# Last stage by seven half-block products (Strassen) over pairs of expert tiles, instead of eight

## The reference, cut to what matters

```python
u = u_emb[e_blk]
a = jnp.einsum('bthkd,btd->bthk', u, h_blk).astype(jnp.float32)
act = (jax.nn.gelu(a) * g_blk).astype(h_blk.dtype)
return jnp.einsum('bthk,bthkd->btd', act, v_emb[e_blk])
```

## Time and profile before

| | us |
|---|---|
| runs | 5167.73, 5172.26, 5175.76 |
| profiled execution, span from first to last instruction | 5167.3 |
| PE busy | 4813.1 (93%) |
| DVE busy | 3059.9 (59%) |
| POOL busy | 1713.3 (33%) |
| ACT busy | 1628.0 (32%) |

### The profile page before, as it was taken

One profiled execution on the slowest core, in us unless ns is written; L12 is line 12 of the kernel. 1 busy time (PEld: TensorE's weight loads), 2 busy tenths in 40 slices (PEclk: granted clock), 3 DMA queues, 4 the chain that ended last, 5 costly groups with the idle time before them and its releaser, 6 DMA issues. The chain is left out here.

```text
span 5167.3 us, 66578 instructions
## 1 busy us (share of the span) xinstructions
PE 4813.1 (93%) x23440; PEld 3844.4 (74%) x23440; DVE 3059.9 (59%) x4062; ACT 1628.0 (32%) x2577; POOL 1713.3 (33%) x818
## 2 busy tenths in 40 slices
PE   6999999967989979999979999999799999999998
PEld 5666666635767758888868888888688888888886
DVE  3777777775423336465578888888544444444444
ACT  2555555553422322222233333332211111111111
POOL 1444444331223112121136666666422222222221
PEclk8999999978999989999989999999899999999999
DMA  2111111104432122222224444444553333434441
GB/s 75 41 44 40 45 46 46 37 25 159 154 122 74 73 87 85 71 89 79 70 90 138 146 146 146 146 144 142 193 193 142 143 142 142 144 146 146 146 143 60
DMA packets 259768, 555.72 MB, mean 108 GB/s; under 512 B 15536, under 2 KB 146864, under 8 KB 257456
## 3 DMA queue, kind: packets, MB, share of 16 engines
q1 hardware_dynamic: 259632, 554.01, 31.1%
HBM read 384.60 MB, written 169.35 MB: 107 GB/s over the span
## 5 line engine op out<-in xcount | busy, mean ns | idle before, releaser
L148 PE MATMUL expert_o<-expert_ahi,expert_vhi 128*128 128x512 f32 x2048 | 798.6, 390 | 34.4 <-POOL expert_vlo L2000 30.0
L150 PE MATMUL expert_o<-expert_ahi,expert_vlo 128*128 128x512 f32 x2048 | 798.1, 390 | 0.0
L149 PE MATMUL expert_o<-expert_alo,expert_vhi 128*128 128x512 f32 x2048 | 798.1, 390 | 0.0
L2052 DVE TENSOR_TENSOR expert_acc<-expert_acc,expert_o 128x512 f32<-128x512 f32 x512 | 352.1, 688 | 736.4 <-PE expert_o L150 732.4
L1386 POOL TENSOR_TENSOR ulo<-uraw,uhi 128x1024 fp32r<-128x1024 f32 x128 | 447.0, 3493 | 770.4 <-ACT uhi L1382 769.6
L2000 POOL TENSOR_TENSOR expert_vlo<-expert_vraw,expert_vhi 128x1024 fp32r<-128x1024 f32 x128 | 323.4, 2527 | 1053.7 <-ACT expert_vhi L2018 1053.7
L148 PE MATMUL spread_a<-hhi,uhi 128*128 128x512 f32 x1280 | 505.7, 395 | 15.1 <-POOL ulo L1386 15.1
L150 PE MATMUL spread_a<-hhi,ulo 128*128 128x512 f32 x1280 | 499.7, 390 | 0.0
L149 PE MATMUL spread_a<-hlo,uhi 128*128 128x512 f32 x1280 | 498.8, 390 | 0.0
L1869 DVE TENSOR_TENSOR spread_gate<-spread_eq,spread_parts 128x2048 bf16<-128x2048 bf16 x128 | 485.1, 3831 | 9.1
L148 PEld LDWEIGHTS expert_o<-expert_ahi,expert_vhi 128*128 128x128 f32 x2048 | 385.2, 188 | 115.9 <-issue 36.2
(11 more groups left out here) (289 smaller groups left out, 9165.8 us busy)
## 6 DMA issues: line engine op xcount, KB each, us to landing
uraw<-in_peer_u SPq DMA_DIRECT2D x128, 512.0 KB, 4.0
gelu_u<-ugelu SPq DMA_DIRECT2D x128, 512.0 KB, 2.9
gates<-spread_stage SPq DMA_DIRECT2D x16, 4096.0 KB, 17.6
expert_act<-gelu_u SPq DMA_DIRECT2D x128, 512.0 KB, 3.6
expert_graw<-gates SPq DMA_DIRECT2D x128, 512.0 KB, 4.4
expert_vraw<-in_peer_v SPq DMA_DIRECT2D x128, 512.0 KB, 6.4
mix_w_raw<-in_w_mix SPq DMA_DIRECT2D x56, 512.0 KB, 3.6
xattn_w_raw<-in_w_cross SPq DMA_DIRECT2D x32, 512.0 KB, 3.5
```

What stands on the lines that cost most here:

```text
L148: nc.tensor.matmul(out, whi, xhi, start=(first and i == 0), stop=False)
L149: nc.tensor.matmul(out, whi, xlo, start=False, stop=False)
L150: mm = nc.tensor.matmul(out, wlo, xhi, start=False, stop=(last and i == len(terms) - 1))
L2052: nc.vector.tensor_tensor(acc[:, k, h * H:h * H + H], acc[:, k, h * H:h * H + H], ops[:, d, h], ALU.add).then_inc(added, 1)
```

## The change

`expert_phase` is rewritten; its host-side layout of the value table changes with it. The stages before it are untouched.

A group is now 8 tiles, as R = 4 pairs of tiles. Of a pair, the even tile and the odd tile are the two halves of the inner dimension. The output width is cut in two (512 each) and the tokens in two (512 each). That makes a 2 by 2 block product of A (values: A11, A12, A21, A22) and B (gated activations: B11 to B22), each block 4 x 128 x 512 numbers. It is done with seven products (Winograd's form), in the order 1, 2, 7, 4, 6, 5, 3, the seven "steps" s = 0 to 6:

- POOL makes four sums of A blocks in place: S3 = A11 - A21, S2 = A22 - S3, S1 = A11 + S2, S4 = A12 - S2.
- DVE makes four sums of B blocks in place: T1 = B22 - B12, T2 = T1 + B11, T3 = T2 - B21, T4 = B22 - T2, beside the four gates.
- A step takes one A block or sum and one B block or sum, in two halves h. For each half ACT makes `ahi` and `bhi`, POOL makes `alo`, DVE makes `blo`; these parts have a ring of 4 halves. PE does 24 matmuls per half (2 r x 4 c x 3 passes), 48 per step, into four of eight banks.
- Each product has an accumulator of its own in `acc`, [P, 7, 4, 512]. DVE adds four banks per step to it (2048 columns in all), during the step after next.
- After the 16th group the seven accumulators are joined by seven adds to four output blocks; the squares and the scaling then go by blocks.

Cut to its core, the diff reads:

```diff
-        E = 4
-        NG = KEYS // E
+        R = 4
+        NG = KEYS // (2 * R)
+        RING = 4
+        STEPS = (1, 2, 7, 4, 6, 5, 3)
+        A_OF = {1: A11, 2: A12, 7: A21, 4: A22, 6: A22, 5: A11, 3: A12}
+        B_OF = {1: B11, 2: B21, 7: B12, 4: B21, 6: B11, 5: B12, 3: B22}
+        A_SUM = {7: 1, 6: 2, 5: 3, 3: 4}
+        B_SUM = {7: 1, 6: 2, 4: 3, 5: 4}
+        GATED = {B21: 1, B11: 2, B12: 3, B22: 4}
...
         def _(sync):
+            load_a(0, 0, A11)
+            load_act(0, B11)
+            load_gate(0, B11)
+            load_act(0, B21)
+            load_gate(0, B21)
+            load_a(0, 0, A12)
+            load_a(0, 0, A21)
+            load_act(0, B12)
+            sync.wait_ge(gated, 1)
+            load_gate(0, B12)
+            load_act(0, B22)
+            sync.wait_ge(gated, 2)
+            load_gate(0, B22)
+            load_a(0, 0, A22)
+            for p, dh, th in ((2, 0, 0), (5, 1, 1), (3, 0, 1), (4, 1, 0)):
+                sync.dma_start(acc[:, p - 1], x_in[:, DC * dh:DC * dh + DC, H * th:H * th + H]).then_inc(x_loaded, 16)
...
         def _(pool):
-            def body(g, par):
-                for q in range(NQ):
-                    pool.wait_ge(vhi_made, g * NQ + (q + 1))
-                    split_low(nc.gpsimd, vlo[:, q], vraw[:, q], vhi[:, q]).then_inc(vlo_made, 1)
+                def s3():
+                    pool.wait_ge(a_loaded[A_SLOT[par][A21]], n * 16 + 16)
+                    nc.gpsimd.tensor_tensor(a21, a11, a21, ALU.subtract).then_inc(s_made, 1)
+                def s2():
+                    pool.wait_ge(alo_made, halves_made(n, 3))
+                    nc.gpsimd.tensor_tensor(a22, a22, a21, ALU.subtract).then_inc(s_made, 1)
...
+                after = {1: s3, 3: s2, 4: s1, 5: s4}
+                for s, p in enumerate(STEPS):
+                    raw = araw[:, A_SLOT[par][A_OF[p]]]
+                    for h in range(2):
+                        i = slot(par, s, h)
+                        pool.wait_ge(ahi_made, n * (2 * NS) + (2 * s + h + 1))
+                        nc.gpsimd.tensor_tensor(alo[:, i], raw[:, PAIRS[h]], ahi[:, i].bitcast(F32), ALU.subtract
+                                                ).then_inc(alo_made, 1)
+                    if s in after:
+                        after[s]()
...
         def _(act):
+                    for h in range(2):
+                        if not first or s >= 2:
+                            if h == 0:
+                                act.wait_ge(half_done, n * NS + (s - 1))
+                            else:
+                                act.wait_ge(bank_done, n * (DC * NS) + DC * (s - 1))
+                        if p in A_SUM:
+                            act.wait_ge(s_made, n * 4 + A_SUM[p])
...
+                        nc.scalar.activation(ahi[:, i], araw[:, A_SLOT[par][a], PAIRS[h]], ACT.Copy).then_inc(ahi_made, 1)
+                        if p in B_SUM:
+                            act.wait_ge(t_made, n * 4 + B_SUM[p])
...
+                        nc.scalar.activation(bhi[:, i], braw[:, b, PAIRS[h]], ACT.Copy).then_inc(bhi_made, 1)
...
         def _(dve):
+                def step0():
+                    gate(n, B12)
+                def step1():
+                    gate(n, B22)
+                    nc.vector.tensor_tensor(b12, b22, b12, ALU.subtract).then_inc(t_made, 1)
+                    if first:
+                        dve.wait_ge(x_loaded, 64)
+                        nc.vector.tensor_tensor(acc[:, 2], acc[:, 2], acc[:, 4], ALU.subtract).then_inc(seeded, 1)
+                def step2():
+                    nc.vector.tensor_tensor(b11, b12, b11, ALU.add).then_inc(t_made, 1)
+                    nc.vector.tensor_tensor(b21, b11, b21, ALU.subtract).then_inc(t_made, 1)
+                def step3():
+                    nc.vector.tensor_tensor(b12, b22, b11, ALU.subtract).then_inc(t_made, 1)
...
+                for s, p in enumerate(STEPS):
+                    for h in range(2):
+                        dve.wait_ge(bhi_made, n * (2 * NS) + (2 * s + h + 1))
+                        nc.vector.tensor_tensor(blo[:, i], braw[:, B_OF[p], PAIRS[h]], bhi[:, i].bitcast(F32), ALU.subtract
+                                                ).then_inc(blo_made, 1)
+                        if h == 0 and s >= 2:
+                            add(n, par, s - 2, first)
+                        elif h == 0 and not first:
+                            add(n - 1, 1 - par, NS + s - 2, False)
+                    if last and s == 4:
+                        nc.vector.tensor_tensor(acc[:, 1], acc[:, 0], acc[:, 1], ALU.add).then_inc(joined, 1)
+                    if s in after:
+                        after[s]()
...
+            join(1, 1, 6, six, 1)
+            join(7, 1, 7, six, 2)
+            join(4, 7, 4, six, 3)
+            add(n, 1, 5, False)
+            join(1, 1, 5, five, 4)
+            join(3, 1, 3, five, 5)
+            join(5, 7, 5, five, 6)
```

More of the change, by code:

```diff
@@ L1927, in expert_phase @@
     with Phase(nc, "expert") as m:
-        E = 4
-        NG = KEYS // E
[L1930 to L1934, removed]
+        R = 4
+        NG = KEYS // (2 * R)
+        DC = NC // 2
+        RING = 4
+        STEPS = (1, 2, 7, 4, 6, 5, 3)
+        NS = len(STEPS)
+        A11, A12, A21, A22 = range(4)
+        B11, B12, B21, B22 = range(4)
+        A_OF = {1: A11, 2: A12, 7: A21, 4: A22, 6: A22, 5: A11, 3: A12}
+        B_OF = {1: B11, 2: B21, 7: B12, 4: B21, 6: B11, 5: B12, 3: B22}
@@ L1969, in _ @@
+        PAIRS = [slice(2 * h, 2 * h + 2) for h in range(2)]
+        OUTPUTS = ((2, 0, 0), (4, 1, 0), (5, 1, 1), (3, 0, 1))
         @block.sync
         def _(sync):
[L1971 to L1986, removed]
-            sync.dma_start(g_sb[:], final_gain).then_inc(c_loaded, 16)
@@ L2037, in _ @@
         @block.vector
         def _(dve):
[L2039 to L2081, removed]
-            dve.wait_ge(c_loaded, 16)
@@ new lines, in add @@
+            def add(n, par, s, first):
+                p, z = STEPS[s], (par + s) % 2 * DC
+                for c in range(DC):
+                    dve.wait_ge(bank_done, n * (DC * NS) + (DC * s + c + 1))
+                    if first and p in (1, 6, 7):
+                        ins = nc.vector.tensor_copy(acc[:, p - 1, c], banks[:, z + c])
+                    else:
+                        ins = nc.vector.tensor_tensor(acc[:, p - 1, c], acc[:, p - 1, c], banks[:, z + c],
+                                                      ALU.subtract if p == 4 else ALU.add)
+                    ins.then_inc(added, 1)
@@ L2105, in _, with body @@
+            def body(n, par, first, last):
+                for s in range(NS):
+                    for h in range(2):
+                        multiply(n, par, s, h, first)
             groups(pe, body)
             pe.wait_ge(ones_made, 1)
-            squares.sum(nc, pe, ones[:])
+            pe.wait_ge(added, DC * (NS * NG - 1))
+            pe.wait_ge(folded, 3)
+            nc.tensor.matmul(banks[:, 0], ones[:], graw[:, 0, 0], start=True, stop=True).then_inc(sum_done[0], 1)
+            pe.wait_ge(squared, 3)
@@ L2110, in build @@
+            for c in range(DC):
+                nc.tensor.matmul(banks[:, 1], ones[:], araw[:, 0, c], start=(c == 0), stop=False)
+            for c in range(DC):
+                pe.wait_ge(square12, c + 1)
+                mm = nc.tensor.matmul(banks[:, 1], ones[:], araw[:, 1, c], start=False, stop=(c == DC - 1))
+            mm.then_inc(sum_done[1], 1)
 def build(nc, a, out):
```

260 lines of the change are left out of this document (190 added, 70 removed).

## The result

The changed kernel takes 5190.04 us (median of 5 runs, 5188.64 to 5194.89) against 5172.26 before: ratio 1.0039, 95% interval 1.0028 to 1.005. It is slower, by 18 us, with an eighth of the last stage's matmuls gone. The forecast was 5193; the profiled span is 5187.6, where the sum said 5188.5.

The account below looks back on a forecast made before the run. It took the queue DVE and POOL share for SBUF-only operations as the bound, 81.6 us a group, 87.5 with waits. 3743 + 2 + 15 x 87.5 + 131 = 5188.5 us span; median 5 above, so 5193, range 5120 to 5250.

Parts of the forecast that it names:

- the shared queue: Last stage: DVE and POOL operations with all inputs in SBUF take turns, 49.3 plus 32.3, together 81.6 us a group.
- holes and starts: Each group: 3.6 us with no request from DVE or POOL, plus 2.3 for operations paying their start in full.
- The group: Last stage, steady group of 8 tiles laid out on paper: 87.5 us, against 87.0 before the change.
- One turn: Step 3: POOL's S2 runs to 48.1 us ahead of DVE's second `blo`, which is held and ends at 49.2.
- empty queue: Before steps 0, 2 and 3, DVE waits 1.2 us for `bhi` and POOL has nothing: 3.6 us a group.
- PE stays the bound: Last stage: DVE and POOL run side by side much of the time; 5022 us; decides below 76 us; chance 0.1.
- The ring of four halves and the banks are never what is waited for: Last stage: PE's waits, 11.4 us a group, never come from operand slots or accumulator banks.
- its idle ending on DVE `blo` and POOL `alo`: Profile after, last stage: PE's idle time should end on the low parts made by DVE and POOL.
- PE's clock: Last stage: clock falls in new waits, alone costing nothing; 1.2 GHz throughout would end at 6160, chance under 0.02.
- the sign said about 1218: Profile after, last stage: PE should be busy about 1218 us of some 1400.
- rows of 2 KB: Start of last stage: if these load at two thirds of the rate, x is ready at 3793, 20 us more.
- the joins meet the fold: Tail: DVE's joins and POOL's fold of squares compete for SBUF turns; if they do not meet, 8 us less.

Follow-up runs that it names:

- the run with two passes: Changed kernel with PE leaving out the third pass (low x high) in the last stage: 5186.78 us, ratio 1.0027 to the kernel before.
- memsets for S: Changed kernel with POOL's four sums S per group not computed, replaced by memsets and adds of 8 columns: 5157.73 us, ratio 0.9971 to the kernel before.
- ACT's order: Changed kernel with ACT making both `ahi` of a step first, then both `bhi`: 5154.54 us, ratio 0.997 to the kernel before.
- both together: Changed kernel with memsets in place of POOL's sums S and ACT making both `ahi` first: 5064.8 us, ratio 0.9796 to the kernel before.

## Why the prediction was right

**The mechanism.** The term that the forecast rests on is the shared queue, at 81.6 us a group against PE's 76.1, and the 5.9 us of holes and starts on top of it. That the two engines share it is shown: T4 takes 6.69 us beside S2 and 2.29 beside memsets, the rest of the kernel being the same. That PE is not the bound is shown by the run with two passes, and that DVE's load is not by the sums moved to DVE. But the queue is not the bound alone. Of the 11.3 us between 87.4 and PE's 76.1, memsets for S win back 2.3, ACT's order 2.5, both together 7.7.

**The group.** 87.5 was forecast, 87.4 measured. Counted from the end of B11's gate (4355.94), `blo` ends at 2.4 and 8.1, 18.0 and 21.6, 28.5 and 34.2, 41.0, as on paper within 0.3 us. One turn differs. In step 3 I let S2 go ahead of the second `blo`, which would end at 49.2; it ended at 44.6. S2 starts 0.17 after POOL's subtraction has ended, since it waits for it, and so loses the turn by 0.12. T4 is then held instead and ends at 51.2, forecast 51.4. The exactness is partly this: while the queue is full, the order of turns moves which operation waits, not the sum.

**How exact the time is.** The 5187.6 for 5188.5 is in part luck. Against the forecast the start was 0.9 us shorter, the fifteen groups 1.5 shorter and the rest 1.5 longer, which nearly cancels; and the stages ahead alone move by up to 7 us from one profiled execution to the next. From the span to the median I added 5 us, as before the change; it was 2.4, which makes 2 of the 3 us between 5193 and 5190.

**The size of the second bound was missed.** The 3.6 us a group of empty queue were named with their cause, the `bhi` that waits for a sum and the `ahi` behind it. But I took that coupling for holes in a full queue. With the queue relieved it still holds the group near 85 us, as the memset run shows (with stand-ins 3 us longer than the sums). The rival "PE stays the bound" was said to decide below 76 us of queue a group; with 64 of queue, by the expectation of that run, it did not come about, and its price, 170 us less, was not to be had by relieving the queue alone.

**Banks.** "The ring of four halves and the banks are never what is waited for" was wrong for the banks. PE waits 87 us in 45 places for the adds (L2179), which DVE does right behind the first `blo` of a step and which free the banks of that same step: PE starts an add, 0.7 us, later than `blo`. So the sign "its idle ending on DVE `blo` and POOL `alo`" did not come, though the adds stand right behind `blo` on the same engine. It cost nothing that a run shows: with a third of its matmuls gone PE waited longer for the same adds, and the time stayed.

**PE's clock.** With the waits it fell: 0.96 over the stage, 404 ns instead of 390 for a matmul. PE is idle 8.1 us of a group's 87.4, not 11.4, because its work got 3 us longer; over the stage it is busy 1283 us, where the sign said about 1218. As forecast, this cost nothing; the run with two passes, at 0.88, shows it again.

**Start and tail.** The seed of x ends at 3771.5, forecast 3772.3. DVE's first gate begins 15.9 us after the first load of the stage is issued, where 16.3 were allowed, so rows of 2 KB did not slow the loads. Once the first group ran, DVE waited 0.2 us for loads in all. From the last matmul to the end are 40.1 us, forecast 39; the joins meet the fold at a cost of 6.8, forecast 8.

**Where the queue's prices come from.** The prices of the queue came from ends of operations in a stage that takes turns, not from means of durations, which mix held and free ones.

## What to carry to other kernels

Ask of every pair of engines what they hold together. If DVE and POOL both work with all inputs in SBUF, add the two up, each at its price when the other stands waiting, and compare the sum, not the larger, with the engine that bounds. The sum is the least it can be: here the waits between the engines put 5.8 us on top of 81.6. Fewer matmuls for more elementwise work is a good trade only if that sum has room. And where one in-order engine feeds two chains, the order on it couples them: it can be a bound of its own just under the first, and the order that helps while one is short can hurt when another is.

## What the hardware showed beyond that

- POOL's memset of 1536 columns neither holds nor is held by DVE's operations with two SBUF inputs (1.37 to 1.40 us in all 192). POOL's add of 8 columns is: 0.20 us alone, up to 2.25 when DVE had the turn, in the same run.
- 2048 fp32 columns on POOL, not in the trace before, cost 4.45 behind DVE's end and 4.59 alone (estimated at 4.48).
- A turn is won by as little as 0.12 us, and it fell the same way in all sixteen groups (T4 took 6690 to 6701 ns): the distance of equal instructions is 87.35 to 87.43 over seven groups.
